# Starting the q products of a decoder layer between the x tiles, behind eight matmuls on zeros

## What is computed

```python
h   = RMSNorm(x) * g_mix
u   = h @ W_in        # -> [pool channels 512 | q 8x64 | k 2x64 | v 2x64]
q   = rmsnorm(q.reshape(B, S, N_HEADS, HEAD_DIM), q_gain)
k   = rmsnorm(k.reshape(B, S, N_KV_HEADS, HEAD_DIM), k_gain)
y_a = PoolMixer(u_pool) @ W_a
y_b = SWA-GQA(q, k, v) @ W_b
x  += (sigmoid(g_a) * y_a + sigmoid(g_b) * y_b) @ W_out
x  += SharedExpert(h2) + RoutedExperts(h2)      # h2 = RMSNorm(x), top 8 of 64 experts
x  += sigmoid(RMSNorm(x) @ W_pg) * RMSNorm(p @ W_pp)
```

## Time and profile before

| | |
|---|---|
| time, median of 3 runs | 988.71 us (987.71 to 989.04) |
| the profiled execution's own time | 985.47 us |
| its span, first to last instruction | 983.6 us |
| mean granted TensorE clock | 0.989 |
| PE busy | 930.8 us, 95% of the span |
| DVE, POOL, ACT busy | 360.6, 229.8, 162.6 us |
| read and written in HBM | 277.16 MB, 29.36 MB |

### The profile page before, as it was taken

One profiled execution on the slowest core, in us unless ns is written; L12 is line 12 of the kernel. 1 busy time (PEld: TensorE's weight loads), 2 busy tenths in 40 slices (PEclk: granted clock), 3 DMA queues, 4 the chain that ended last, 5 costly groups with the idle time before them and its releaser, 6 DMA issues.

```text
span 983.6 us, 15583 instructions
## 1 busy us (share of the span) xinstructions
PE 930.8 (95%) x6327; PEld 477.3 (49%) x6327; DVE 360.6 (37%) x773; ACT 162.6 (17%) x304; POOL 229.8 (23%) x345
## 2 busy tenths in 40 slices
PE   6999999999999999999999999999879898997698
PEld 4678788888655533333333333333323333332345
DVE  5565673336436743333332111111101111111787
ACT  2001324210011211111111111111101111221021
POOL 4115923162110212222222222211211111101110
PEclk9999999999999999999999999999979999999899
DMA  9930005421393659999999999999999999999972
GB/s 331 332 129 1 1 1 175 167 86 51 131 382 154 214 209 397 398 416 403 406 418 409 409 420 413 419 420 422 412 422 423 419 422 411 420 404 365 379 279 86
DMA packets 81816, 298.95 MB, mean 304 GB/s; under 512 B 9251, under 2 KB 33863, under 8 KB 57552
## 3 DMA queue, kind: packets, MB, share of 16 engines
q1 hardware_dynamic: 68048, 261.09, 67.2%
q0 software_dynamic: 11920, 33.63, 8.7%
q10 hardware_dynamic: 1776, 3.21, 0.9%
HBM read 277.16 MB, written 29.36 MB: 312 GB/s over the span
## 4 chain that ended last, share of the span: by engine, by line
PE 74%; DMA 20%; SPq 3%; DVE 2%; issue 1%; ACT 1%; POOL 0%; POOLq 0%; ACTq 0%
PE ps L2196 23%; DMA ring<-in_w_exp_up 16%; PE ps L1807 12%; PE ps L2225 9%; PE ps L1957 6%; PE ps L1936 5%; PE ps L2340 4%; PE ps L1763 3%; PE ps L1740 2%; SPq L463 2%; PE ps L2012 1%; PE ps L1769 1%; DMA ring<-accumulator 1%; PE ps L2205 1%; DMA accumulator<-actT,stage 1%; SPq L517 1%
## 5 line engine op out<-in xcount | busy, mean ns | idle before, releaser
L2196 PE MATMUL ps<-ring,gates 128*32 128x512 f32 x2560 | 287.7, 601 | 25.4 <-DMA ring<-in_w_exp_up 24.7
L2196 PEld LDWEIGHTS ps<-ring,gates 128*32 128x32 f32 x2560 | 88.0, 111 | 217.3 <-issue 216.4
L2225 PE MATMUL ps<-ring,poolbuf 128*32 128x512 f32 x1280 | 145.6, 595 | 3.1 <-DMA ring<-in_w_exp_down 3.1
L1554 DVE COPY poolbuf<-ps 128x256 f32<-128x256 f32 x40 | 17.0, 425 | 352.7 <-PE ps L2205 352.7
L2225 PEld LDWEIGHTS ps<-ring,poolbuf 128*32 128x32 f32 x1280 | 37.9, 109 | 83.9 <-issue 82.2
L784 POOL COPY stage<-qT 128x1 uint32<-128x1 uint32 x40 | 7.2, 180 | 261.1 <-PE ps L1740 233.4
L971 ACT ACTIVATE actT<-ps,qT 128x1024 f32<-128x1024 f32 x40 | 44.5, 1113 | 142.3 <-PE ps L2225 142.3
L963 ACT ACTIVATE poolbuf<-ps 128x256 f32<-128x256 f32 x40 | 15.3, 384 | 277.5 <-PE ps L2196 277.5
L1807 PE MATMUL ps<-xrow,ring 128*128 128x256 f32 x256 | 57.9, 381 | 0.1
L1957 PE MATMUL ps<-ring,gates 128*128 128x512 f32 x128 | 56.4, 594 | 0.0
L1740 PE MATMUL ps<-cst,rows 128*128 128x128 f32 x352 | 48.5, 285 | 7.8 <-DVE rows L1067 7.7
(11 more groups left out here) (288 smaller groups left out, 1069.6 us busy)
## 6 DMA issues: line engine op xcount, KB each, us to landing
ring<-in_w_exp_down SPq DMA_DIRECT2D x64, 1024.0 KB, 17.3
ring<-in_w_exp_gate SPq DMA_DIRECT2D x62, 1024.0 KB, 14.0
ring<-in_w_exp_up SPq DMA_DIRECT2D x62, 1024.0 KB, 15.7
ring<-accumulator SPq DMA_DIRECT2D x12, 1024.0 KB, 13.0
ring<-in_w_gate SPq DMA_DIRECT2D x8, 1024.0 KB, 10.3
ring<-in_w_in SPq DMA_DIRECT2D x5, 1024.0 KB, 12.9
xrow<-in_x SPq DMA_DIRECT2D x8, 512.0 KB, 5.2
accumulator<-ring SPq DMA_DIRECT2D x1, 4096.0 KB, 19.8
```

The costliest lines, as they stand in the source:

```text
L2196: last = mm(bank(2 + k)[part, :], hgT[k][:, q, part], pair_view(EXPERT_SLOT[js[c]])[:, q], start=(q == 0), stop=(q == KD - 1))
L2225: last = mm(bank(6 + half)[part, :], eactT[r % 2][:, q, part], w[:, q, half * 512:(half + 1) * 512], start=(q == 0), stop=(q == 1))
```

## The change

It has four parts.

1. DVE's program begins with setting a 128x512 tile to zero (the first part of `gates`, not yet used), and PE's with `WARM` = 8 products of 128x512 on that tile into bank 7, whose result nobody reads. They stand ahead of the first transpose.
2. SP issues x0, q0, x1, q1, x2, x3, kv in place of x0 to x3, q0, q1, kv.
3. PE's order: the q product of tile 0 is split in two halves of 256 columns, each waiting for its own weight unit; the transposes of tile 1 stand between them, and those of tiles 2 and 3 behind the q product of tile 1. The k and v product of tile 0 comes behind these, that of tile 1 next, and then `qk_T(0)`. `qkv_ps` becomes `q_ps` and `kv_ps`, and the ring slots of q0 and q1 are given free by `q_ps`.
4. DVE's order: `first_rows` and `first_T` of tile 0, then of tile 1, then `first_rows` of tiles 2 and 3, then `first_T` of tiles 2 and 3.

```diff
+WARM = 8
+        idle_tile = gates[:, 0, :]
-            released_by = {"q0": (qkv_ps, 2 * NT), "q1": (qkv_ps, 2 * NT), "kv": (qkv_ps, 2 * NT)}
+            released_by = {"q0": (q_ps, NT), "q1": (q_ps, NT), "kv": (kv_ps, NT)}
...
             for i in range(NT):
                 sp.dma_start(xrow[:, i, :], x_rows[i]).then_inc(x_loaded[i], 16)
-            for u in range(3):
-                load_dense(u)
+                if i < 2:
+                    load_dense(i)
+            load_dense(2)
...
-            for i in range(NT):
-                first_rows(i)
-                if i:
-                    first_T(i - 1)
-            first_T(NT - 1)
+            nc.vector.memset(idle_tile, 0.0).then_inc(idle_tile_ready, 1)
+            first_rows(0)
+            first_T(0)
+            first_rows(1)
+            first_T(1)
+            first_rows(2)
+            first_rows(3)
+            first_T(2)
+            first_T(3)
...
-            pe.wait_ge(act_moved, 16)
-            for i in range(NT):
+            def first_T(i):
                 pe.wait_ge(rows_ready, i + 1)
                 strided_T(rows[:, i, :], i, 2 * i, P, hT_ps)
 
+            pe.wait_ge(idle_tile_ready, 1)
+            for _ in range(WARM):
+                mm(bank(7), idle_tile[:, 0:P], idle_tile, start=True, stop=True)
+            pe.wait_ge(act_moved, 16)
...
+                for c0, c1 in halves:
+                    if i == 0:
+                        loaded(f"q{c0 // 256}")
+                    w = qv[:, :, c0 // 256] if c1 - c0 == 256 else qv
+                    for k in range(KD):
+                        last = mm(bank(2 * (i % 2))[:, c0:c1], actT[:, k, i * P:(i + 1) * P], w[:, k],
+                                  start=(k == 0), stop=(k == KD - 1))
...
+            first_T(0)
+            q_product(0, ((0, 256),))
+            first_T(1)
+            q_product(0, ((256, 512),))
+            q_product(1)
+            first_T(2)
+            first_T(3)
+            kv_product(0)
             for i in range(NT):
-                qkv(i)
+                if i >= 2:
+                    q_product(i)
                 if i:
+                    kv_product(i)
                     qk_T(i - 1)
```

More of the change, by code:

```diff
@@ L303, in build @@
         vec_ps, vec_ready = sem("vec_ps"), sem("vec_ready")
-        qkv_ps, q_copied, kv_copied = sem("qkv_ps"), sem("q_copied"), sem("kv_copied")
+        idle_tile_ready = sem("idle_tile_ready")
+        q_ps, kv_ps, q_copied, kv_copied = sem("q_ps"), sem("kv_ps"), sem("q_copied"), sem("kv_copied")
         qk_ssq, qk_rstd, qk_normed = sem("qk_ssq"), sem("qk_rstd"), sem("qk_normed")
@@ L867, in _ @@
             for i in range(NT):
-                act.wait_ge(qkv_ps, 2 * i + 1)
+                act.wait_ge(q_ps, i + 1)
                 nc.scalar.activation(rows[:, i, 0:QD], bank(2 * (i % 2)), ACT.Copy).then_inc(q_copied, 1)
@@ L1146, in _ @@
             for i in range(NT):
-                dve.wait_ge(qkv_ps, 2 * i + 2)
+                dve.wait_ge(kv_ps, i + 1)
                 nc.vector.tensor_copy(rows[:, i, QD:QD + 2 * KVD], bank(2 * (i % 2) + 1)[:, 0:2 * KVD]
@@ L1742, in strided_T, with q_product, kv_product @@
                     last.then_inc(done, 1)
-            pe.wait_ge(act_moved, 16)
-            for i in range(NT):
+            def first_T(i):
                 pe.wait_ge(rows_ready, i + 1)
                 strided_T(rows[:, i, :], i, 2 * i, P, hT_ps)
+            pe.wait_ge(idle_tile_ready, 1)
+            for _ in range(WARM):
+                mm(bank(7), idle_tile[:, 0:P], idle_tile, start=True, stop=True)
+            pe.wait_ge(act_moved, 16)
             qv = pair_view(DENSE_SLOT[DENSE_AT["q0"]])
             kvv = unit_view(DENSE_SLOT[DENSE_AT["kv"]], KD)
-            def qkv(i):
+            def q_product(i, halves=((0, 512),)):
                 pe.wait_ge(hT_ready, 2 * i + 2)
[L1754 to L1758, removed]
                 if i >= 2:
                     pe.wait_ge(q_copied, i - 1)
[L1761 to L1765, removed]
+                for c0, c1 in halves:
[5 more added lines that the diff above has]
+                                  start=(k == 0), stop=(k == KD - 1))
+                if c1 == 512:
+                    last.then_inc(q_ps, 1)
+            def kv_product(i):
                 if i == 0:
                     loaded("kv")
+                if i >= 2:
+                    pe.wait_ge(kv_copied, i - 1)
                 for k in range(KD):
@@ L1770, in qkv @@
                               start=(k == 0), stop=(k == KD - 1))
-                last.then_inc(qkv_ps, 1)
+                last.then_inc(kv_ps, 1)
             def qk_T(i):
```

## The result

| | before | changed |
|---|---|---|
| median | 988.21 us (6 runs) | 996.37 us (6 runs) |
| lowest, highest | 986.34, 990.13 | 995.17, 997.58 |
| profiled execution: time, span | 985.47, 983.6 | 996.27, 994.4 |

A forecast was written before the change was run, and what follows sets the result against it. PE was taken to bound the kernel, with no idle time from the first pool product to make good a late start. A 7.1 us delay plus 2.1 us of low clock gave 988.7 + 9.2 = 997.9 us, range 994.3 to 1000.7.

The forecast's parts named there:

- The bound: From the first pool product on PE has no idle time, so a late start reaches the end nearly whole.
- rival in which the DMA-bound stage takes it up: From 600 to 900 us, PE waits 9 us less for experts' weights; the end stays at 988.7; chance 0.05.
- The zeros: At PE's start, eight products on zeros run from 1.4 to 11.0, 3.3 us after transposes could start before.
- rival that zeros don't raise the clock: At PE's start, zeros last until 15.2 and transposes and first q start slow: 16.1 us slower, 1004.8; chance 0.06.
- The loads: At the start, the new order of x and q loads costs and gains nothing; PE is later than all.
- DVE's new place: Ahead of `qk_T(0)`, block sums wait for the last copies; PE idles 6.1 us, delay 7.1 us.
- The clock behind the stall: After PE's idle time at `qk_T(0)`, the clock falls to half and costs 2.1 us, ends 0 and 2.7.
- rival in which the clock stays high: Behind `qk_T(0)`, the stall comes but the clock does not fall: 7.1 us slower, 995.8; chance 0.12.
- The sum: Whole kernel: 7.1 + 2.1 = 9.2 us slower, 997.9 us against the median.

The follow-up runs named there:

- the first trace: The profiled execution of the changed kernel, unedited, in its first comparison with the kernel before: 996.27 us; that comparison's ratio is 1.0078.
- transposes ahead: Changed kernel, all eight zeros kept, with transposes of tiles 2 and 3 and k and v of tile 0 before q of tile 1: ratio 1.0021.
- the second: The changed kernel run once more without edits, beside the kernel before, and its trace: ratio 1.0097.
- without the zeros: Changed kernel without the eight products on zeros and without the zeroed tile: ratio 1.0085 to the kernel before.
- Zeros in the stall: Changed kernel with five more products on zeros between the k and v product of tile 1 and `qk_T(0)`: ratio 1.0061.
- three zeros: Changed kernel with transposes of tiles 2 and 3 and k and v of tile 0 before q of tile 1, and `WARM = 3`: ratio 0.9985.

## Why the prediction was right, step by step

**The bound.** Right. In the first trace the delay was 9.6 us at the first pool product and 9.6 at the output projection. The rival in which the DMA-bound stage takes it up did not happen: 10.4 us at the last expert product.

**The zeros.** Forecast: start at 1.4, end at 11.0. Measured: 1.44 and 11.28 in the first trace, and 9.96 to 11.47 over seven. The low clock of the start was put at the 5.4 us of the kernel before; with zeros it lasted 3.2 to 6.2 us, so the mechanism is right and that the first trace came within 0.3 us is luck in part. The rival that zeros don't raise the clock fell in the first trace: the zeros' sixteen passes took 9.8 us, not 13.8; the first started 0.85 us apart, the last 0.43. The Trainium skill, "TensorE: Matmul & The Clock Gate", section "What's actually happening", says that the gate is set by how busy PE has been recently, and these runs agree for an operand of all zeros.

**The loads.** Right in that they were on no path: with eight zeros PE was later than all of them.

**DVE's new place.** The step that carried the forecast. `qk_T(0)` was put at 42.7 and came at 42.13, against 35.5 before on the same view: 6.7 us late where 7.1 stood. Most of the difference is the copies of tiles 2 and 3, put at 2.9 us and measured at 2.4 (28.68 to 31.08). Moving one block of PE's program took the whole wait away (transposes ahead), and filling it with the q product did so too. By that the cause is shown, from two sides.

**The clock behind the stall.** The mechanism was right, the term too small: 2.1 us forecast, 2.95 in the first trace (26.05 against 23.1 us from `qk_T(0)` to the pool products before), 2.3 in the second, 1.7 without the zeros. Zeros in the stall gave the whole of it back, so the clock and not the wait for DVE costs this part. The rival in which the clock stays high did not occur: the clock fell in all five traces with a stall there, down to the one of 2.4 us.

**The sum.** 6.7 + 2.9 = 9.6 us in the profiled execution, against 9.2; in the second one, 7.6 us. The two comparisons of times give 7.7 and 9.6 (0.97% of 988.1). The forecast lies among these, and its distance of 0.4 us from the first trace means little.

## What to carry to other kernels

When a block of work is moved on one engine, look at what the other engine does only after its result: here PE gave DVE the last transposed tiles one q product later, and DVE's 11 us of sums and norm were left with 6.9 us of cover. Work on zeros that raises the clock was worth 2.6 to 3.1 us in the traces, as long as it ended before the real data was there; beyond that it pays back what it gains: three products gained, eight did not. A stall on PE is to be priced with the low clock behind it; here that added 1.7 to 2.9 us to stalls of 2.4 to 5.3.

## What the runs showed of the hardware

DVE's block sums, additions and subtractions that read two SBUF operands, slow POOL down. POOL's scaling and power of 128x10 elements took 0.21 and 1.98 us with DVE quiet and 1.11 and 2.94 us beside the block sums, on the same program otherwise. The Trainium skill, "SBUF — State Buffer", section "Who interferes with whom", states that a DVE instruction with two SBUF inputs contends with a GpSimd instruction that reads SBUF; the runs agree, with these numbers. Whether it takes two operands was not tested, and the kernel before has a case with one: POOL's L691 on 128x1 elements took 0.38 and 0.53 us beside DVE's scaling of a 128x1024 tile (L1067), and 0.19 with DVE idle; both times it ended 0.05 us behind DVE's operation. A gap of DVE's that is a wait for POOL is thus no free room for such work.

In the start of the kernel the granted clock fell to 0.50 (1.2 GHz) around idle times of PE of 5.3, 4.3 and 2.4 us, and stayed at 1.00 through idle times of 0.95 us (zeros in the stall) and 1.43 us (three zeros). From `qk_T(0)` to the pool products each fall cost 1.7 to 2.9 us. The length of the idle time does not decide alone: late in the trace of the kernel before, 2.64 us ahead of 732.68 were followed by 3.4 us at 0.50, and 2.77 us ahead of 933.36 were followed by full clock. So what the 2.4 us did in one execution need not happen in each. At the very start the profile's clock column reads 1.00 although the passes run at half pace; only the spacing of the instructions tells.
